# Two transformer blocks in one program: modulation sums moved to VectorE turns, the norms at the seam made per tile, second-block weights fetched before the seam

## What is computed

```
x = first_block(x, ...)            # 2 layers: rms_norm, wide projection, MLA attention, dilated attention, out-projection
                                   # and a last rms_norm(x, final_g)
x = second_block(x, c, ctx, ...)   # 2 layers of: adaln modulation, mixer, expert mixture
...
def adaln(cond, mod_w, mod_b):
    m = silu(cond) @ mod_w + mod_b          # 6 * 1024 numbers for each layer
    return split(m, 6)                      # shift1, scale1, gate1, shift2, scale2, gate2
a  = rms_norm_2(h_lat, norm1_g) * (1 + scale1) + shift1     # input of the mixer, in transposed form
ac = the same for the 256 context rows, with the numbers of c_ctx
y  = even_mixer(a, ac, ...)        # projection to q, k, v and a pooled part, head norms, rope, attention
h_lat = h_lat + gate1 * y ; h_lat = h_lat + gate2 * hier_moe(...)
```

## Time and profile before

| | |
|---|---|
| median of 3 runs | 2244.4 us (2242.2 to 2245.37) |
| the profiled execution: its time / its span | 2244.1 us / 2242.5 us |
| PE busy | 2044.5 us, 91% |
| DVE, ACT, POOL busy | 35%, 26%, 32% |
| mean granted TensorE clock | 0.951 |
| transfers | 339.29 MB, mean 151 GB/s |

### The profile page before, as it was taken

The page is one execution under the profiler, slowest core; times in us unless marked ns, Lnnn a source line. Parts: engine busy times, 40 slices in busy tenths (PEclk is TensorE's granted clock), DMA queues, the critical chain, the costliest instruction groups (busy, mean ns, idle before and its releaser), DMA issues. The chain is left out here.

```text
span 2242.5 us, 23210 instructions
## 1 busy us (share of the span) xinstructions
PE 2044.5 (91%) x7824; PEld 1099.2 (49%) x7824; DVE 794.9 (35%) x1596; ACT 580.6 (26%) x1205; POOL 715.6 (32%) x1055
## 2 busy tenths in 40 slices
PE   7999999999999999999997697995999699778995
PEld 5555555555564555555542355653444344344442
DVE  1434534432123444433315358533222300442223
ACT  3234331234113442221511114521111211111110
POOL 4766766756766676600000031000110100001101
PEclk9999999999999999999998798996999799878997
DMA  7234343234343244360112600016995621055994
GB/s 301 84 113 150 133 145 119 95 127 145 127 150 111 90 166 144 119 266 38 48 75 104 220 16 22 1 46 279 349 366 210 226 75 38 0 226 227 369 366 165
DMA packets 71119, 339.29 MB, mean 151 GB/s; under 512 B 8760, under 2 KB 10230, under 8 KB 56694
## 3 DMA queue, kind: packets, MB, share of 16 engines
q1 hardware_dynamic: 38502, 217.48, 25.7%
q0 software_dynamic: 27920, 103.82, 13.1%
q10 hardware_dynamic: 4608, 16.78, 1.8%
HBM read 292.97 MB, written 45.09 MB: 151 GB/s over the span
## 5 line engine op out<-in xcount | busy, mean ns | idle before, releaser
L386 PE MATMUL psA<-gB,ring 128*128 128x512 f32 x1024 | 455.1, 597 | 0.0
L324 POOL TENSOR_TENSOR wm<-wm,cs 128x256 f32<-128x256 f32 x448 | 266.3, 627 | 135.4 <-DMA wm<-in_mod_w 134.8
L386 PEld LDWEIGHTS psA<-gB,ring 128*128 128x128 f32 x1024 | 189.5, 190 | 223.8 <-issue 223.8
L328 POOL TENSOR_TENSOR wm<-wm 128x256 f32<-128x256 f32 x336 | 243.8, 753 | 31.1 <-issue 23.1
L378 PE MATMUL psA<-ring,gB 128*128 128x384 f32 (+1 forms) x768 | 242.9, 474 | 1.2 <-ACT gB L665 1.2
L378 PEld LDWEIGHTS psA<-ring,gB 128*128 128x128 f32 x768 | 144.6, 190 | 92.0 <-issue 6.8
L1326 POOL DMA_INDIRECT arena<-xs_scratch,idx x4 | 3.9, 965 | 446.7 <-issue 446.7
L842 DVE COPY probT<-psT 128x512 f32<-128x512 f32 x96 | 65.9, 686 | 159.4 <-PE psT L367 159.4
L1460 PE MATMUL psSO<-wreg,arena 128*128 128x512 f32 x256 | 115.3, 593 | 1.9 <-DVE arena L1986 1.9
L1445 PE MATMUL psA<-wreg,arena 128*128 128x512 f32 x256 | 114.9, 602 | 0.0
L1402 PE MATMUL psA<-wreg,mixT 128*128 128x512 f32 x256 | 113.1, 602 | 1.6 <-issue 0.8
(11 more groups left out here) (283 smaller groups left out, 2790.6 us busy)
## 6 DMA issues: line engine op xcount, KB each, us to landing
wm<-in_mod_w POOLq DMA_DIRECT2D x56, 1024.0 KB, 7.9
wreg<-in_w_gu SPq DMA_DIRECT2D x16, 2048.0 KB, 8.6
wreg<-in_w_dn SPq DMA_DIRECT2D x32, 1024.0 KB, 12.3
ring<-in_w_qk SPq DMA_DIRECT2D x24, 1024.0 KB, 4.9
mixT<-in_w_gu SPq DMA_DIRECT2D x8, 2048.0 KB, 8.6
aT<-in_w_gu SPq DMA_DIRECT2D x8, 2048.0 KB, 8.5
ys_scratch<-arena ACTq DMA_DIRECT2D x32, 512.0 KB, 9.9
ring<-in_w_v SPq DMA_DIRECT2D x8, 1536.0 KB, 6.9
```

The lines of the kernel that those rows point to most:

```text
L324: nc.gpsimd.tensor_tensor(wm[:, b, k], wm[:, b, k], c_all[:, k].to_broadcast([P, MCH]), ALU.mult)
L328: nc.gpsimd.tensor_tensor(wm[:, b, k], wm[:, b, k], wm[:, b, n + k], ALU.add)
L386: m = nc.tensor.matmul(psA[:, n % 2, :], w(i), src[:, k, :], start=(i == 0), stop=(i == len(ks) - 1))
```

## The change

The two blocks return their engine streams and one `nc.Block()` runs the first block's stream and then the second's on each engine, with no meeting between. All large buffers are cut from one tensor, `pool_mem`, so the second block's can lie where the first block's are free already. (In the rows of the instruction order these buffers all read `pool_mem`.)

- **Sums.** `fold_columns` and `summed_columns` (DVE): 20 times, DVE turns 128x512 of `macc` in 32x32 squares (STREAM_TRANSPOSE) and reduces over 32, which leaves 16 columns in `parts`; four matmuls on PE with `fold` (a 0/1 matrix) add the four groups of 32 partitions for all. Ten of the 20 stand in the gaps of hp = 3 in layer 1, ten between the adds of the last out-projection.
- **Row order.** In layer 1 `x` goes through `x1` early (16 stores, 4 loads) and `mixT` is written in the plain token order (`spread`), so the last out-projection already has the second block's tiles.
- **Norms per tile.** After each tile's adds DVE makes the final norm and the next first norm of that tile; PE turns tile 0 ahead of the last tile's out-projection and does the queries' projection between the other tiles' turns.
- **Loads.** `even_w_in` comes in three parts (`w_q`, `w_kv`, `w_p`), the first during hp = 3; the context and `macc` are also fetched before the seam.
- **Gates.** The eight gate rows (16 matmuls) stand behind the pooled projection, with four banks.
- The cast of the mask is made in eight instructions where it was two.

```diff
+            def fold_columns():
+                dve.wait_ge(m_stored, 16 * (MACC // MCH))
+                nc.vector.memset(fold[:, :, :], 0.0)
+                dve.drain()
+                for c in range(4):
+                    for b in range(4):
+                        own, here = slice(32 * b, 32 * b + 32), slice(32 * c, 32 * c + 32)
+                        nc.vector.tensor_copy(fold[own, c, here], ident[own, own])
+            def summed_columns(i):
+                p = i // 4
...
+                if i % 4 == 0:
+                    dve.wait_ge(macc_loaded[p % 2], 16 * (p // 2 + 1))
+                start = 2048 * (p % 2) + 512 * (i % 4)
+                dve.drain()
+                nc.vector.transpose(swapped, wm_flat[:, start:start + 512])
+                dve.drain()
+                m = nc.vector.tensor_reduce(parts[:, 16 * i:16 * i + 16], swapped.rearrange("p (a n) -> p a n", n=32), AX.X, ALU.add)
+                if i % 4 == 3:
+                    m.then_inc(summed, 1)
...
+                        if L + 1 == DEPTH and hp == 3:
+                            if t == 0:
+                                fold_columns()
+                            for i in ((0, 1, 2), (3, 4, 5), (6, 7), (8, 9))[t]:
+                                summed_columns(i)
...
+            for t in range(3):
+                added(t, 0)
+                if t == 0:
+                    summed_columns(10)
+                added(t, 1)
+                for i in ((11, 12), (14, 15), (17, 18))[t]:
+                    summed_columns(i)
+                final_norm(t)
+                summed_columns((13, 16, 19)[t])
+                keep["norm_residual"](dve, 0, t)
+            added(3, 0)
+            dve.wait_ge(folded, 1)
...
+            m.then_inc(mod_ready, 1)
+            dve.drain()
+            keep["modulated_high"](dve, 0, 0, 0, 0, 0)
+            added(3, 1)
+            keep["modulated_high"](dve, 0, 1, 0, 0, 0)
+            final_norm(3)
+            keep["norm_residual"](dve, 0, 3)
```

```diff
+                        if L + 1 == DEPTH and (t, half) == (3, 0):
...
+                            keep["turn_tile"](pe, 0, 0, 0)
+                        if L + 1 == DEPTH and (t, half) == (3, 1):
+                            pe.wait_ge(summed, PIECES)
+                            for c in range(4):
+                                m = nc.tensor.matmul(psSO[:, 0, 0:16 * PIECES], fold[:, c, :],
...
-            turn_norm(0, 0)
-            pe.wait_ge(n_xn, N_CTX + CT)
-            for k in range(KD):
-                turn(T_CTX + k, [cxn[:, t, tile(k)] for t in range(CT)])
-            pe.wait_ge(wi_loaded, 16)
-            pe.wait_ge(t_copied, KD)
+            turn_tile(0, 0, 1)
+            project_even(0)
+            turn_tile(0, 0, 2)
+            project_even(1)
+            turn_tile(0, 0, 3)
+            project_even(2)
+            project_even(3)
...
+            for i in range(8):
+                if i >= 4:
+                    pe.wait_ge(gb_copied, i - 3)
+                nc.tensor.matmul(psSO[:, i % 4, :], ones[:], gate_sums[:, 512 * i:512 * i + 512], start=True, stop=False)
```

More of the change, by code:

```diff
@@ L1218, in rows, with on, keep_it, tile @@
         return ap.rearrange("a p k n -> p (a k) n")
-    with nc.Block() as block:
-        @block.sync
+    keep.update(w_q=w_q, w_kv=w_kv, w_p=w_p, cx=cx, mbrow=mbrow)
+    engines = {}
+    def on(name):
+        def keep_it(f):
+            engines[name] = f
+            return f
+        return keep_it
+    def tile(t):
+        return slice(t * P, (t + 1) * P)
+    def turn_blocks(pe, n, blocks):
+        if n >= 2:
+            pe.wait_ge(t_copied, n - 1)
+        for t, b in enumerate(blocks):
+            i = nc.tensor.transpose(psT[:, n % 2, t * P:(t + 1) * P], b, ident[:])
+        i.then_inc(t_ready, 1)
@@ new lines, in turn_rows_of, with mean_square, square_tile @@
+    def turn_rows_of(pe, first, norm, t):
+        pe.wait_ge(n_xn, norm + t + 1)
+        for half in range(2):
+            turn_blocks(pe, first + 2 * t + half, [xm[:, t, tile(4 * half + k)] for k in range(4)])
+    def mean_square(act, i, src, junk, done):
+        nc.scalar.activation(junk, src, ACT.Square, accum_out=ss2[:, i:i + 1])
+        act.drain()
+        nc.scalar.activation(rms2[:, i:i + 1], ss2[:, i:i + 1], ACT.Sqrt, scale=1.0 / D, bias=eps[:]).then_inc(done, 1)
+    def square_tile(act, t):
+        act.wait_ge(xf_ready, t + 1)
+        mean_square(act, t, h[:, t, :], xm[:, t, :], n_rms)
@@ new lines, in square_context, with modulated_low @@
+    def square_context(act):
+        act.wait_ge(cx_loaded, 16)
+        for t in range(CT):
+            mean_square(act, NT + t, cx[:, t, :], context_junk, c_rms)
+    def modulated_low(act, first, t, mul, shift):
+        act.wait_ge(t_ready, first + 2 * t + 1)
+        for k in range(4):
+            m = nc.scalar.activation(aT[:, k, tile(t)], psT[:, 0, tile(k)], ACT.Identity,
+                                     scale=amul[:, mul, k:k + 1], bias=mT[:, shift + k:shift + k + 1])
+        m.then_inc(t_low, 1)
@@ new lines, in modulated_high, with norm_tile @@
+    def modulated_high(dve, first, t, mul, shift, lows):
+        dve.wait_ge(t_ready, first + 2 * t + 2)
+        for k in range(4, KD):
+            if k == KD - 1:
+                dve.wait_ge(t_low, lows + t + 1)
+            m = nc.vector.tensor_scalar(aT[:, k, tile(t)], psT[:, 1, tile(k - 4)],
+                                        amul[:, mul, k:k + 1], mT[:, shift + k:shift + k + 1], ALU.mult, ALU.add)
+        m.then_inc(t_copied, 2)
+    def norm_tile(dve, norm, i, src, out, ready, count):
+        dve.wait_ge(ready, count)
+        nc.vector.reciprocal(rs2[:, i:i + 1], rms2[:, i:i + 1])
+        dve.drain()
+        nc.vector.tensor_scalar(out, src, rs2[:, i:i + 1], None, ALU.mult).then_inc(n_xn, 1)
@@ new lines, in _ @@
+            turn_tile(0, 0, 1)
[5 more added lines that the diff above has]
+            project_even(3)
+            pe.wait_ge(wi_loaded[1], 16)
+            for t in range(NT):
+                fill(A_KV + t, 256, [(aT[:, k, tile(t)], w_kv[:, k, :]) for k in range(KD)])
+                if t == 0:
+                    pe.wait_ge(n_xn, N_CTX + CT)
+                for k in (2 * t, 2 * t + 1):
+                    turn(T_CTX + k, [cxn[:, c, tile(k)] for c in range(CT)])
@@ L1613, in _ @@
             experts(1)
-        @block.scalar
+        @on("scalar")
         def _(act):
@@ L2171, in _ @@
                 combine(1, t)
+    return engines
 def layouts(inputs):
```

506 lines of the change are left out of this document (266 added, 240 removed).

## The result

| | before | after |
|---|---|---|
| median, runs of both kernels on one chip | 2244.9 us (2242.2 to 2251.9) | 2188.3 us (2187.1 to 2197.6) |
| profiled execution: time / span | 2244.1 / 2242.5 us | 2187.1 / 2185.1 us |
| ratio to before, 95% interval | | 0.975 [0.973, 0.978] |
| mean granted clock | 0.951 | 0.957 |

The change makes the kernel 56.6 us faster. The prediction was 2171 with 2164 to 2184 around it, so some 16 us of the forecast gain are missing (73.3 us were forecast, the spans of the two profiled executions differ by 57.4), and the time lies above the range.

What follows compares the result with a forecast made beforehand. PE was taken to bound the kernel wherever it has work, the gain being its idle time at the seam: 73.9 + 1.0 - 1.3 - 0.3 = 73.3 us off 2244.1, so 2171 us, range 2164 to 2184.

Steps and rivals of the forecast that it cites:

- sums at 1.55 us: Each DVE sum, a turn in squares and a reduction, was taken at 1.55 us, with bounds 1.4 to 3.0.
- copies dearer than 0.11: Sign of a wrong forecast: PE waits over 2 us in hp = 3 because the 32x32 copies cost more than 0.11.
- up to hp = 3 (mask casts): MLA part: six more mask-cast instructions cost DVE some 0.5 us, of which 0.3 was let reach PE.
- hp = 3, copies and sums: Ahead of tile 1, three sums, memset and 16 copies need 7.0 us against 5.7 to give; PE waits 1.3.
- PE's work from the end of piece (2,1) to the keys' turn: Stretch over the seam: 113.6 us of PE work at full clock where it took 187.5, so 73.9 us earlier.
- of it the eight gate rows: Behind the pooled projection, ahead of the keys' turn: 2.1 us each, 16.8 together.
- of it `fold`, and waits: At the seam: 1.0 us for the matmuls with fold, and PE waiting for nothing there.
- turns of keys and queries: Behind the gate rows: all 22 blocks run at full clock as PE comes without a pause, 1.0 us of gain.
- theory A: Experiments' theory: the missing 16 us are mostly 1.2 GHz time, from the hp = 3 wait and gate rows with one-row matmuls.
- The sums were not slow (1): Rival 1: DVE sums take 3.0 us, costing 16 us instead of 1.3 in hp = 3 and out-projection, 2186; chance 0.10.
- the stepped writes do not show (2): Rival 2: each stepped mixT write takes 0.7 us more and all reaches PE, 8 us, 2179; chance 0.05.
- no new wait at the seam (3): Rival 3: tile 0's chain, the reload of x or a macc piece late by 5 to 12 us, 2176 to 2183; chance 0.12.

Runs made afterwards that it cites:

- fold_and_bias: Against the changed kernel, POOL makes fold and adds the gates' bias rows, so PE's gate rows are 8 matmuls; 2167.4 us, ratio 0.9656.
- sums_twice: Against the changed kernel, each of the 20 sums on DVE is made twice over; 2210.5 us, ratio 0.9847.
- fold_on_pool: Against the changed kernel, the memset and 16 copies that make fold move from DVE to POOL; 2181.3 us, ratio 0.9708.
- plain_writes: Against the changed kernel, layer 1 writes mixT contiguously in row order, which gives another output; 2212.5 us, ratio 0.9856.
- weights_late: Against the changed kernel, the three parts of even_w_in are fetched behind the wait for the last sum; 2189.2 us, ratio 0.9751.

## Why the prediction was wrong

The direction was right, and so was most of the mechanism: no idle time of PE above 2 us at the seam, gate rows ahead of the keys' turn, sums at 1.55 us. DVE waits for PE ahead of four of the eight adds, not of all. Two of the prediction's signs failed: the granted clock is not 1.00 up to the keys' turn, and PE waits more than 2 us in hp = 3, which it had named as the sign of copies dearer than 0.11. Of the terms, each in us of gain or of PE's time:

| step | forecast | measured |
|---|---|---|
| up to hp = 3 (mask casts) | -0.3 | -0.9, with 1.9 us between runs of the same code |
| hp = 3, copies and sums | -1.3 | -5.9: 2.5 for the wait (0.185 us a copy), 1.1 for ACT's late copy, 2.3 at the 1.2 GHz level |
| PE's work from the end of piece (2,1) to the keys' turn | 113.6 | 120.4 (1172.70 to 1293.07) |
| of it the eight gate rows | 16.8 | 22.4 (five at 2.1, three at 4.0) |
| of it `fold`, and waits | 1.0 and 0 | 1.1, and 0.83 + 0.87 of waits |
| turns of keys and queries | +1.0 | +0.3, at the low clock |
| the rest of the kernel | 0 | -3.1 (883.5 to 886.6 from the first scores on) |

The differences add up to 15.8 us, and about 8.6 of them are time at the 1.2 GHz level (5.6 in the gate rows, 2.3 in hp = 3, 0.7 in the turns): more than half, but not nearly all, of what theory A says.

The failed step is "the eight gate rows: two of them start 2.0 us apart ..., so 2.1 each, 16.8". The price was read from rows that stand between stretches of full products, and carried over to eight in succession as if the clock could not fall while PE is busy. The trace of before already showed that it can. This is its timeline around the second and behind the fourth group of two gate rows in succession:

```profile
1204.86 1.02 PE L632 MATMUL psA<-wm,ones 128*128 128x512 f32 x2
...
1206.86 1.13 PE L632 MATMUL psA<-wm,ones 128*128 128x512 f32 x2
1207.91 1.12 PE L633 MATMUL psA<-mixT,ones 1*128 1x512 f32 x2
1208.97 3.64 PE L639 MATMUL psSO<-wm,ones 128*128 128x512 f32 x4
...
1225.91 5.40 PE L639 MATMUL psSO<-ring,ones 128*128 128x512 f32 x8
```

Two products (four records) take 3.64 us there where two took 1.88 at 1212.44, with no gap ahead of them, and the granted clock is 0.50 from 1209 to 1212. It is 0.50 again from 1226 to 1228, behind the fourth group, and stays up behind the first and the third. The row that the prediction read (1197.21) is of the first. So the gate rows had done before what they do after, and a price from one group without a fall could not show it.

The second failed step is hp = 3. "I take 0.11 for a copy" priced a 32x32 copy by adds of 128x16; it is 0.185, which made the wait 2.35 us instead of 1.3. The larger part was not in the sum at all: about 3.4 us behind a wait of 2.35 (5.8 came back with fold on POOL), some 1.1 of it ACT's table load and gate activation, which the lateness put onto PE's path, and 2.3 the lower clock. The Trainium skill (TensorE: Matmul & The Clock Gate, "HAM oscillation — how this bites in real kernels") describes a kernel in which waits for transfers make the work behind them start at the lower clock. The traces agree for the waits of 4.97 us (fold_and_bias, where the six blocks of the keys' turn behind it take 1.54) and 6.98 us (sums_twice, 1.54 too). Behind the 2.35 us the six blocks still took 0.88, and the clock fell only after them. The fall in the gate rows has no such wait ahead of it.

The rest of PE's work was right to within 0.7 us. The turned tiles account for about that much: a tile was priced at 1.07 us, the length of its row, and takes 0.87 from its start to the next start (1172.70 to 1173.58 is one).

Of the rivals none came. The sums were not slow (1), the stepped writes do not show (2), and there was no new wait at the seam (3). From the Trainium skill's figure for a stepped destination (Vector Engine (DVE) Microarchitecture Reference, "Measured stream behaviour on trn2") the prediction had estimated about 1.4 us for one. Measured are 1.02 to 1.05, some 0.35 above the plain one; the step here is 16 words and not the 24 of the page, and the measurement decides.

The last 3.1 us, behind the first scores, stay open. Over ten profiles of kernels whose code is the same there this stretch takes 882.5 to 888.3 us, and before has 883.5, so I take it for scatter, of which nothing more was shown. Also open is why the clock falls at a different place in the gate rows each time: 10.4 us behind the first row (twice), 6.3, and 4.1 (twice), and not at all behind some groups of two. It makes the kernel's own runs scatter, and a single profile can't price it.

## What to carry to other kernels

When matmuls are moved, read the granted clock behind them as well as their duration: here alternating products with one row of input kept PE busy by the profile, and the clock fell all the same. Price work at its own neighbours' clock only if the neighbours move with it. A wait that opens on PE in a dense stretch can cost more than it shows (here 5.8 us for 2.35), through the clock and through the other engines that come late with it; the wait of 4.97 us ahead of the attention, which has waits of its own, cost about 1. So a cheap operation on a tight engine belongs on an idle one (POOL made `fold` in 4.4 us for which nobody waited), and a bias row is better added by an idle engine to one partition of the sums than by a matmul of its own.

## What the runs showed that was not expected

- Granted clock at 0.50 over 12 to 24 us in which the profile shows PE busy throughout: products of 128x512 alternating with 1x512 (changed kernel, fold_on_pool, plain_writes, sums_twice, weights_late). Sixteen of 128x512 in its place: 1.00.
- An alternating pair is also dearer at the full clock, 1.05 us a product against 0.86 in a row of full ones.
- A late operation on DVE reached PE a second time through ACT, whose table load (1.28 us) had stood in an idle stretch before and now stood on the path.
- Sixteen 32x32 copies on DVE, 2.96 us; on POOL 3.89 us.
- STREAM_TRANSPOSE of 128x512 in SBUF: 0.71 us, near the 0.74 of a shuffle.
- POOL's add of 2048 numbers on one partition: 4.7 us (9.40 for two).
